# One-core hybrid block (gated delta rule + sparse attention + SwiGLU): five pieces of work moved or reshaped

## Chip, cores, metric

The kernel runs on one core of one Trainium2 chip. The metric is the device time of one execution in microseconds (us). Before the change it is 573.63 us, the median of three runs (571.04 to 574.39 us).

## The reference

One layer of a decoder block on x of shape (1, 256, 1024), float32. Two token mixers read the same normed input, their outputs are gated and merged, and a SwiGLU follows:

```python
h = rmsnorm(x, norm1_w)
proj = h @ w_in                      # one wide projection, cut into the parts of all heads
y_a = gated_deltanet(...)            # conv, l2-normed q/k, chunked delta rule, gated rmsnorm
y_b = native_sparse_attention(...)   # compressed, selected and window branches, shared bias
mixed = sigmoid(gate_a) * (y_a @ w_proj_a) + sigmoid(gate_b) * (y_b @ w_proj_b)
x = x + mixed @ w_out
h2 = rmsnorm(x, norm2_w)
x = x + (silu(h2 @ w_gate) * (h2 @ w_up)) @ w_down
```

What matters below: the attention's queries (8 heads of 128) are rmsnormed per token and head; the delta rule needs the inverse of unit-triangular 128x128 matrices, 16 of them (8 heads, two token tiles); the bias of the attention is a function of the distance of two tokens, one table per head; the delta rule's output o is rmsnormed per token and head.

## The kernel before, in words

**Weights as a stream.** All weights pass through SBUF in chunks of 1 MB (`CHUNKS`: gk, gq, gv 0..3, kc, vc, cmpk 0..3 mixed with nq 0..3, ks, kw, cmpv 0..3 mixed with vs, vw, gz, and so on to gu and dn). SyncE's queue issues the loads in that order into `raw` buffers (three in a ring, and `raw_ahead` for nq0 and nq2); a load waits until the chunk that held its buffer has been used. Each float32 chunk is split in two: ScalarE (ACT) copies it to `w_hi` (L629), VectorE (DVE) forms `w_lo = raw - w_hi` (L982), and TensorE (PE) does three products per tile (L1467 to L1469). There are two pairs `w_hi`/`w_lo`, so a chunk can be split only when the chunk two before it has been used by PE. Chunks of cmpk and cmpv are used unsplit (L1548).

**Slots.** Each engine runs its own list in program order, written out by hand: one slot per chunk, with two halves. In a slot, beside the chunk's own products, stand small pieces: a stage of the delta rule over four blocks b of four problems (`STAGE_AT`: row, kt, vt, knT, gram, kq, X4 ... o1; three banks in a ring carry the results between PE and DVE or ACT), a unit of the attention's softmax (`unit`), turns (transposes on PE) and norms. Semaphores couple the engines; a wait holds everything behind it on its engine.

**The diagonal blocks of the inverse.** After stage gram, GpSimd (POOL) sends the 16x16 diagonal blocks through DRAM (`sub_a`, `sub_m`), DVE inverts them (`solve_diagonal`, two parts), POOL sends them back (`sub_d`, `sub_dt`) and spreads them into `Db` and `DTb` by 16 DMAs (L589, L590). Stage X4, in the slot of cmpv0, waits for all of these.

**The bias.** DVE makes the table `bias_v` (8 x 384) in the opening. POOL writes it out 32 times to DRAM (`bias_rows`, L560), and reads it back skewed as `bias_g` (128 x 8 x 256, L576, four DMAs of 256 KB). It is first read much later, in the slot of vw.

**The queries.** The chunks nq0..3 are narrow: PE holds 128 weight columns and streams the 256 tokens of h, so the result stands head by head with tokens along the row. ACT copies it to `nqT` (L716) and squares it (L718). The sums of squares come from PE (`head_sums`, j = 2): four products with ones (L1661) after half 0 of ks, a copy by ACT (`csum_n`, L941), four turns after half 1 of ks. DVE makes the factor `rn` in the slot of cmpv1. Chunks of WIDE_KINDS (gz and later) are wide instead: PE holds 128 tokens of h and streams 512 weight columns; the token tile is the half.

**Opening.** x is normed (DVE, ACT), turned into channels (PE, eight tiles k), h is split tile by tile, and the first chunk's products run behind it.

**The factor of o.** DVE sums the squares of o (`output_sums`, L1144) in the slot of mga1, half 0, and makes the factor (`output_factor`) in half 1; then POOL scales o by it and by the gate (`scale_o`, L596 and L601), four blocks of each.

**End.** Four pieces of 512 columns of the output, each a DVE instruction (L1459) and a DMA on SyncE's queue.

Of the kernel before, what the change touches and what calls it, by code (L numbers as in the profile page):

```python
# [76 lines left out]
WIDE_KINDS = ("gz", "mga", "pa", "mgb", "pb")  # L77
# [116 lines left out]
def hybrid_block(nc, x, norm1_w, w_in, conv_w, a_log, dt_bias, gdn_norm_w, cmp_pe, cmp_w1, cmp_w2,  # L194
# [5 lines left out]
    with ctx:  # L200
# [33 lines left out]
        ones_nq = at("ones_nq", yb_at + 11 * KB + 128, [P, 32])  # L234
# [14 lines left out]
        nsq = [ar(5, f"nsq{i}", (P, 2, SEQ), off=i * 2 * KB) for i in range(4)]  # L249
# [44 lines left out]
        csum_n = at("csum_n", cursor[0] - 2 * KB, [P, 2 * SEQ])  # L294
# [55 lines left out]
        xss, xn_done = sem("xss"), sem("xn_done")  # L350
# [39 lines left out]
        def wait_bank(eng, n, t=0):  # L390
# [89 lines left out]
        def _(sp):  # L480
# [30 lines left out]
            for i in range(4):  # L511
                sp.wait_ge(fin, i + 1)
                t, c = i // 2, i % 2
                sp.dma_start(out[0].rearrange("(t p) d -> p t d", p=P)[:, t, c * 512:(c + 1) * 512],
                             out_sb[:, t, c * 512:(c + 1) * 512]).then_inc(out_done, 16)
            sp.wait_ge(out_done, 64)

        @block.gpsimd
        def _(pool):
# [87 lines left out]
        def _(act):  # L607
# [280 lines left out]
            for n in range(len(CHUNKS) + 1):  # L888
# [37 lines left out]
                for half in range(2):  # L926
# [10 lines left out]
                    for name in slot_stages(n, half):  # L937
                        gdn(name)
# [994 lines left out]
```

## Time and profile before

| | |
|---|---|
| median of the runs | 573.63 us |
| the profiled execution | 575.51 us, its span 573.7 us |
| mean granted TensorE clock | 0.993 of full speed |
| PE busy (matmul) | 563.1 us, 98% |
| DVE busy | 387.2 us, 67% |
| ACT busy | 305.1 us, 53% |
| POOL busy | 70.7 us, 12% |
| PE's share of the chain that ended last | 91% |

How to read it: the span runs from the first to the last instruction, and the execution has 1.8 us outside it. PE is busy nearly throughout, so the interesting things are the few microseconds in which it isn't, and those in which it is busy at a lower clock. A matmul's shown duration is longer than its step, since matmuls are pipelined; the step is read from the distance of starts, or from the chain, whose pieces do not overlap.

### The profile page before, as it was taken

The page shows a single profiled execution, that of the slowest core. Times are in us where ns is not written, and L with a number is a line of the kernel's source. Part 1 is how long each engine was busy: PE and PEld are TensorE (multiplying, and loading weights), DVE is VectorE, ACT ScalarE, POOL GpSimd, SP SyncE. Part 2 cuts the span into 40 slices and gives each one's busy share as a digit, 9 for nine tenths or more (in the row PEclk, how much of TensorE's full clock was granted, in tenths as well). Part 3 has the DMA queues.
Part 4 walks back from the last instruction along what each step waited for, and adds up shares of the span by engine and source line. Part 5 has one row for each costly group of instructions (what it writes and reads, how often), then busy time and mean ns, then how long its engine had stood idle before and what let it go on. Part 6 is the DMA issues. An engine that isn't in the chain of part 4 may idle for free.

```text
span 573.7 us, 9788 instructions
## 1 busy us (share of the span) xinstructions
PE 563.1 (98%) x3894; PEld 496.6 (87%) x3894; DVE 387.2 (67%) x617; ACT 305.1 (53%) x490; POOL 70.7 (12%) x85
## 2 busy tenths in 40 slices
PE   8999999999799999999999999999999999999997
PEld 8999999899698888888888888898888888888886
DVE  5879978846466653699875574757766656666664
ACT  4768568623345646655563634366555454554542
POOL 3122210964600000005200000000000000000000
PEclk9999999999799999999999999999999999999999
DMA  7944586289934433442354456575476665657631
GB/s 259 286 148 148 161 223 220 68 258 238 271 126 167 140 128 108 147 146 76 107 189 142 146 161 208 155 199 165 149 218 171 197 202 171 199 168 214 181 114 73
DMA packets 99254, 98.17 MB, mean 171 GB/s; under 512 B 4818, under 2 KB 83591, under 8 KB 99210
## 3 DMA queue, kind: packets, MB, share of 16 engines
q1 hardware_dynamic: 96896, 93.63, 52.7%
q0 software_dynamic: 1808, 2.78, 2.4%
q10 hardware_dynamic: 506, 1.14, 0.6%
q8 instruction: 31, 0.51, 0.4%
q14 instruction: 13, 0.11, 0.1%
HBM read 96.39 MB, written 1.84 MB: 171 GB/s over the span
## 4 chain that ended last, share of the span: by engine, by line
PE 91%; DVE 3%; DMA 3%; ACT 1%; issue 1%; ACTq 0%; DVEq 0%
PE ps L1467 18%; PE ps L1469 17%; PE ps L1468 17%; PE ps L1573 14%; PE ps L1576 7%; PE ps L1472 4%; PE ps L1693 4%; DMA raw<-in_w_in 2%; PE ps L1842 2%; PE ps L1816 2%; PE ps L1548 1%; PE ps L1718 1%; DMA rows_b<-in_cmp_pe 1%; DVE w_lo L982 1%; PE ps L1727 1%
## 5 line engine op out<-in xcount | busy, mean ns | idle before, releaser
L982 DVE TENSOR_TENSOR w_lo<-raw,w_hi 128x2048 fp32r<-128x2048 f32 x75 | 173.1, 2308 | 94.8 <-ACT w_hi L629 94.7
L629 ACT ACTIVATE w_hi<-raw 128x2048 fp32r<-128x2048 f32 x75 | 143.4, 1911 | 77.1 <-PE ps L1469 68.1
L1573 PE MATMUL ps<-h_both,w_hi 128*128 128x512 f32 x352 | 122.7, 397 | 0.2 <-issue 0.2
L1576 PE MATMUL ps<-h_both,w_lo 128*128 128x256 f32 x352 | 91.4, 280 | 0.3 <-DVE h_both L1008 0.3
L1467 PE MATMUL ps<-h_both,w_hi 128*128 128x256 f32 x272 | 77.8, 286 | 0.2 <-issue 0.2
L1468 PE MATMUL ps<-h_both,w_hi 128*128 128x256 f32 x272 | 76.9, 283 | 0.0
L1469 PE MATMUL ps<-h_both,w_lo 128*128 128x256 f32 x272 | 76.9, 283 | 0.0
L1573 PEld LDWEIGHTS ps<-h_both,w_hi 128*128 128x128 f32 x352 | 63.9, 188 | 13.8 <-issue 1.4
L1576 PEld LDWEIGHTS ps<-h_both,w_lo 128*128 128x128 f32 x352 | 66.4, 189 | 4.0 <-issue 0.6
L1467 PE MATMUL ps<-w_hi,h_both 128*128 128x512 f32 (+1 forms) x160 | 59.3, 370 | 3.1 <-issue 3.0
L1469 PE MATMUL ps<-w_hi,h_both 128*128 128x512 f32 (+1 forms) x160 | 56.7, 354 | 0.0
L1468 PE MATMUL ps<-w_lo,h_both 128*128 128x512 f32 (+1 forms) x160 | 56.6, 354 | 0.0
L1467 PEld LDWEIGHTS ps<-h_both,w_hi 128*128 128x128 f32 x272 | 52.1, 192 | 2.6 <-issue 2.5
L1468 PEld LDWEIGHTS ps<-h_both,w_hi 128*128 128x128 f32 x272 | 52.1, 192 | 0.0
L1469 PEld LDWEIGHTS ps<-h_both,w_lo 128*128 128x128 f32 x272 | 52.1, 192 | 0.0
L1467 PEld LDWEIGHTS ps<-w_hi,h_both 128*128 128x128 f32 x160 | 31.4, 196 | 8.7 <-issue 4.7
L1090 DVE SCALAR_TENSOR_TENSOR cacc<-cin,cols_a,cacc 128x256 f32<-128x256 f32 x72 | 35.0, 553 | 0.0
L1469 PEld LDWEIGHTS ps<-w_hi,h_both 128*128 128x128 f32 x160 | 31.4, 196 | 4.1
L1467 PE MATMUL ps<-w_hi,g_hi 128*128 128x512 f32 x88 | 34.4, 390 | 0.0
L1469 PE MATMUL ps<-w_hi,g_lo 128*128 128x512 f32 x88 | 34.3, 390 | 0.0
L1468 PEld LDWEIGHTS ps<-w_lo,h_both 128*128 128x128 f32 x160 | 31.5, 197 | 3.3
L1468 PE MATMUL ps<-w_lo,g_hi 128*128 128x512 f32 x88 | 34.3, 389 | 0.0
(381 smaller groups left out, 959.4 us busy)
## 6 DMA issues: line engine op xcount, KB each, us to landing
raw<-in_w_in SPq DMA_DIRECT2D x31, 1024.0 KB, 5.3
raw<-in_w_gate SPq DMA_DIRECT2D x22, 512.0 KB, 3.9
raw<-in_w_up SPq DMA_DIRECT2D x22, 512.0 KB, 5.2
raw<-in_w_down SPq DMA_DIRECT2D x11, 1024.0 KB, 4.9
raw<-in_cmp_w SPq DMA_DIRECT2D x8, 1024.0 KB, 7.3
raw<-in_w_proj_a SPq DMA_DIRECT2D x4, 1024.0 KB, 5.5
raw<-in_w_proj_b SPq DMA_DIRECT2D x4, 1024.0 KB, 5.0
raw<-in_w_out SPq DMA_DIRECT2D x4, 1024.0 KB, 5.1
```

Source lines behind the costliest of these rows:

```text
L629: nc.scalar.activation(w_hi[s % NSPL][:], raw[RAW_OF[n]][:], ACT.Copy).then_inc(hi_done, 1)
L982: nc.vector.tensor_tensor(w_lo[s % NSPL][:], raw[RAW_OF[n]][:], w_hi[s % NSPL][:].bitcast(f32), ALU.subtract).then_inc(lo_done, 1)
L1090: ins = nc.vector.scalar_tensor_tensor(acc, src[:, a, j:j + SEQ], tap(k, a, j), acc, ALU.mult, ALU.add)
L1467: pe.matmul(bank, lhs(lh), rhs(rh), start=start, stop=False)
L1468: pe.matmul(bank, lhs(lh), rhs(rl), start=False, stop=False)
L1469: return pe.matmul(bank, lhs(ll), rhs(rh), start=False, stop=stop)
L1472: return pe.transpose(o, i, ident[0:n, 0:n])
L1573: cross = lambda stop: pe.matmul(banks[part][:], hi[:, k, part * P:(part + 1) * P], h_both[:, :, k, :], start=(k == 0), stop=stop)
L1576: end = pe.matmul(banks[part][:, 0:SEQ], lo[:, k, part * P:(part + 1) * P], h_hi[:, k, :], start=False, stop=False)
L1693: mm = lambda q, lhsT, rhs, start=True, stop=True: pe.matmul(b4[:, q, :], lhsT, rhs, start=start, stop=stop)
L1816: last = pe.matmul(log_ps[:, a * SEQ:a * SEQ + w], nqT[:, h, t * P:(t + 1) * P], keys[:, h // 4, 0:w], start=True, stop=True)
L1842: last = pe.matmul(o, values[:, k, g, :], pt[j % 2][:, a * (t + 1) + k, :], start=False, stop=(a == 1 and k == t))
```

## The change

1. **Bias.** The write of `bias_rows` moves ahead, behind the squares of k and q; the four reads into `bias_g` move behind the 16 DMAs of the inverse's diagonal blocks.
2. **Queries.** nq becomes wide: the result stands token by token in PSUM. ACT squares it head by head with a running sum straight into `rn`'s column (L745 of the changed kernel, four instructions per half) and copies it to `nq_tok`; PE turns it back (`turn_q`, 16 turns in all, after nq2 and after ks), ACT copies the turned banks to `nqT` (`turned_q`). The head sums with j = 2 go (four products, four turns, the copy `csum_n`).
3. **Opening.** The second token tile's norm is cut by columns: 0 to 511 on ACT, 512 to 1023 on DVE behind the copy of `cols_b`; the turns of k = 0..3 wait for the first half alone. The first chunk's split of tiles 0..3 is cut in two.
4. **Factor of o.** `output_sums` moves from (mga1, half 0) to (gz3, half 1), `output_factor` from (mga1, 1) to (mga1, 0).
5. **Last turn of k.** Block 3 of stage kt moves from half 0 to half 1 of its slot, ahead of vt.
6. **End.** The last 512 columns of the output go out in two pieces of 256.

The diff, cut to its core:

```diff
-WIDE_KINDS = ("gz", "mga", "pa", "mgb", "pb")
+WIDE_KINDS = ("nq", "gz", "mga", "pa", "mgb", "pb")
...
+    name = STAGE_AT[where]
+    if name == "kt":
+        return [("kt", range(NB - 1))]
+    return ([("kt", (NB - 1,))] if name == "vt" else []) + [(name, range(NB))]
...
+OUT_PIECES = [(0, slice(0, 512)), (0, slice(512, 1024)), (1, slice(0, 512)), (1, slice(512, 768)), (1, slice(768, 1024))]
+TURN_Q = {(AT["nq", 2], 1): 0, (AT["ks", 0], 1): 1}
...
             act.wait_ge(rstd_ready, 1)
-            nc.scalar.activation(xn_sb[:, 1, 512:], x_sb[:, 1, 512:], ACT.Copy, scale=scol["x"][:, 5:6]).then_inc(xn_done, 1)
+            nc.scalar.activation(xn_sb[:, 1, 0:512], x_sb[:, 1, 0:512], ACT.Copy, scale=scol["x"][:, 5:6]).then_inc(xn_done, 1)
             act.wait_ge(raw_first, 16)
-            nc.scalar.activation(w_hi[0][:, 0:KT // 2, :], raw[0][:, 0:KT // 2, :], ACT.Copy).then_inc(first_hi, 1)
+            nc.scalar.activation(w_hi[0][:, 0:2, :], raw[0][:, 0:2, :], ACT.Copy).then_inc(first_hi, 1)
             for k in range(KT):
+                if k == 2:
+                    nc.scalar.activation(w_hi[0][:, 2:KT // 2, :], raw[0][:, 2:KT // 2, :], ACT.Copy).then_inc(first_hi, 1)
...
-                elif kind == "nq":
-                    nc.scalar.activation(nqT[:, 2 * i:2 * i + 2, :], bank, ACT.Copy).then_inc(copied, 1)
-                    act.wait_ge(copied, COPY_NO[n] + 1)
-                    nc.scalar.activation(nsq[i][:], nqT[:, 2 * i:2 * i + 2, :], ACT.Square).then_inc(nq_sq, 1)
...
+                if kind == "nq":
+                    act.wait_ge(half_done, 2 * n + 1 + t)
...
+                    for q in range(4):
+                        h = 2 * (i - 1) + q
+                        nc.scalar.activation(sc[0][:, q // 2, q % 2 * P:(q % 2 + 1) * P], bank[:, q * P:(q + 1) * P], ACT.Square,
+                                             accum_out=col["rn"][:, h, t:t + 1]).then_inc(nq_sq, 1)
+                    nc.scalar.activation(nq_tok[i // 2][:, t, :], bank[:], ACT.Copy).then_inc(copied, 1)
...
+            def turned_q(p):
+                for c in range(2):
+                    act.wait_ge(nq_turned, 2 * p + c + 1)
+                    nc.scalar.activation(nqT[:, 4 * p + 2 * c:4 * p + 2 * c + 2, :].rearrange("p h c -> p (h c)"), (log_ps, pv_ps)[c][:],
+                                         ACT.Copy).then_inc(nq_out, 1)
...
+                    if half == 0 and (n - 1, 1) in TURN_Q:
+                        turned_q(TURN_Q[n - 1, 1])
...
-                    if (n, half) == (AT["ks", 0], 1):
-                        act.wait_ge(csum_mm, 3)
-                        nc.scalar.activation(csum_n[:], ps[5][:], ACT.Copy).then_inc(csum_out, 1)
...
-            nc.vector.tensor_scalar(xn_sb[:, 1, 0:512], x_sb[:, 1, 0:512], scol["x"][:, 5:6], None, ALU.mult).then_inc(xn_done, 1)
             dve.wait_ge(pre_pe, 2)
             nc.vector.tensor_copy(cols_b[:], ps[7][:, P:P + NROWS]).then_inc(pre_dve, 1)
+            nc.vector.tensor_scalar(xn_sb[:, 1, 512:], x_sb[:, 1, 512:], scol["x"][:, 5:6], None, ALU.mult).then_inc(xn_late, 1)
...
+                    if (n, half) == (AT["gz", 3], 1):
+                        output_sums()
                     if (n, half) == (AT["mga", 1], 0):
-                        output_sums()
-                    if (n, half) == (AT["mga", 1], 1):
                         output_factor()
...
-            pe.wait_ge(xn_done, TT + 1)
-            to_channels(xn_sb, range(KT), tr_ready)
+            pe.wait_ge(xn_done, TT)
+            to_channels(xn_sb, range(KT // 2), tr_ready)
+            pe.wait_ge(xn_late, 1)
+            to_channels(xn_sb, range(KT // 2, KT), tr_ready)
...
+            def turn_q(p):
+                pe.wait_ge(copied, COPY_NO[AT["nq", 2 * p + 1]] + 1)
...
+                for c in range(2):
+                    if p == 1:
+                        pe.wait_ge(nq_out, c + 1)
+                    for q in range(4):
+                        h, t = 2 * c + q // 2, q % 2
+                        last = transpose((log_ps, pv_ps)[c][:, q * P:(q + 1) * P], nq_tok[p][:, t, h * P:(h + 1) * P])
+                    last.then_inc(nq_turned, 1)
...
                 elif m == W2_K:
                     pe.wait_ge(hid_done, 1)
-                    pe.wait_ge(rk_ready, 1)
+                    pe.wait_ge(nq_out, 4)
```

**POOL's queue around the diagonal blocks.** `sub_m` is the last step of the way out, the DMAs of `Db` and `DTb` are the way back. Before:

```order
L560 DMA bias_rows<-bias_v 256x1x384
L561 MEMSET DTb 128x2048
L564 TENSOR_TENSOR kn<-kn,cols 128x512 x4
L571 DMA sub_a<-ATb 16x16x16 x8
L573 DMA sub_m<-sub_a 128x256
L576 DMA bias_g<-bias_rows 32x8x256 x4
L578 DMA cmp_136<-in_cmp_w 128x4x128
L581 MEMSET Db 128x2048
L583 DMA sub_d<-sub_t 128x256
L585 DMA sub_dt<-sub_tt 128x256
```

After (the cut leaves out 14 DMAs of `Db` and `DTb` like the two shown):

```order
L563 MEMSET DTb 128x2048
L566 TENSOR_TENSOR kn<-kn,cols 128x512 x4
L573 DMA sub_a<-ATb 16x16x16 x8
L575 DMA sub_m<-sub_a 128x256
L577 DMA cmp_133<-in_cmp_w 128x4x128
L580 MEMSET Db 128x2048
L582 DMA sub_d<-sub_t 128x256
L584 DMA sub_dt<-sub_tt 128x256
...
L588 DMA Db<-sub_d 16x16x16
L589 DMA DTb<-sub_dt 16x16x16
L591 DMA bias_g<-bias_rows 32x8x256 x4
```

The four reads of the bias no longer stand between `sub_m` and the load of `cmp`; they are behind the last pair of `Db` and `DTb`, and the write of `bias_rows` has left this stretch.

**ACT from the split of nq3 (`w_hi_53<-raw_49`) to `hid_tok`.** The row `w_hi_52<-raw_51` is the split of ks, the next `w_hi_53<-raw_49` that of kw. Before:

```order
L629 ACTIVATE w_hi_53<-raw_49 128x2048
L716 ACTIVATE nqT<-ps 128x512
L718 ACTIVATE nsq_89<-nqT 128x512
L629 ACTIVATE w_hi_52<-raw_51 128x2048
L716 ACTIVATE nqT<-ps 128x512
L718 ACTIVATE nsq_90<-nqT 128x512
L629 ACTIVATE w_hi_53<-raw_49 128x2048
L936 ACTIVATE hid_tok<-ps 128x256
```

After:

```order
L631 ACTIVATE w_hi_53<-raw_49 128x2048
L631 ACTIVATE w_hi_52<-raw_51 128x2048
L769 ACTIVATE nqT<-ps 128x512 x2
L745 ACTIVATE sc_127,cols<-ps 128x128 x4
L747 ACTIVATE nq_tok_87<-ps 128x512
L745 ACTIVATE sc_127,cols<-ps 128x128 x4
L747 ACTIVATE nq_tok_87<-ps 128x512
L631 ACTIVATE w_hi_53<-raw_49 128x2048
L955 ACTIVATE hid_tok<-ps 128x256
```

Between the split of ks and that of kw stood two instructions; now twelve stand there (two copies of turned banks, twice four squares with a sum and a copy).

**DVE around the sums of o's squares, in the slot of mga1.** Before:

```order
L1276 TENSOR_TENSOR sc_131<-sc_131,s_fac 128x2x128
L1144 TENSOR_REDUCE cols<-kn 128x4 x4
L1265 SCALAR_TENSOR_TENSOR sc_130<-ps,cols,bias_g 128x2x128
L1266 TENSOR_REDUCE s_nm<-sc_130 128x2
L1273 RECIPROCAL s_fac<-s_se 128x2
L1274 TENSOR_TENSOR s_fac<-s_fac,gates 128x2
L1276 TENSOR_TENSOR sc_135<-sc_135,s_fac 128x512
L982 TENSOR_TENSOR w_lo_55<-raw_51,w_hi_53 128x2048
L1003 TENSOR_SCALAR cols<-cols 128x16
```

After:

```order
L1294 TENSOR_TENSOR sc_128<-sc_128,s_fac 128x2x128
L1019 TENSOR_SCALAR cols<-cols 128x16
...
L1283 SCALAR_TENSOR_TENSOR sc_127<-ps,cols,bias_g 128x2x128
L1284 TENSOR_REDUCE s_nm<-sc_127 128x2
L1291 RECIPROCAL s_fac<-s_se 128x2
L1292 TENSOR_TENSOR s_fac<-s_fac,gates 128x2
L1294 TENSOR_TENSOR sc_132<-sc_132,s_fac 128x512
L998 TENSOR_TENSOR w_lo_55<-raw_51,w_hi_53 128x2048
L1283 SCALAR_TENSOR_TENSOR sc_128<-ps,cols,bias_g 128x512
```

The ten small instructions of the factor, which begin with L1019, stand where the sums stood, one unit and one split earlier than before, so POOL's scaling of o may begin that much earlier.

## Rows read from the trace of the kernel before

**Rows 1.** Page, part 1: busy us, share of the span, instructions
```profile
PE 563.1 (98%) x3894; PEld 496.6 (87%) x3894; DVE 387.2 (67%) x617; ACT 305.1 (53%) x490; POOL 70.7 (12%) x85
```

**Rows 2.** PE's waits: line, releaser, us in total, times, longest
```profile
PE ps L1467 <- issue: 3.2, 2, 3.0
...
PE ps L1472 <- DVE sc L1276: 1.0, 1, 1.0
...
PE ps L1472 <- DVE AXb L1114: 0.6, 1, 0.6
```

**Rows 3.** Chain that ended last: start us, us, what
```profile
79.51 0.99 PE ps L1661 x8
...
114.99 3.77 PE ps L1693 x32
130.26 1.04 PE ps L1548 x16
131.32 11.22 DMA raw<-in_w_in
142.57 1.92 ACT w_hi L629
144.49 2.48 issue
...
152.43 1.33 PE ps L1661 x8
...
165.64 2.01 PE ps L1718 x64
...
340.40 0.87 PE ps L1472 x8
363.10 0.87 PE ps L1472 x8
```

**Rows 4.** Windows: PE, PEld, DVE, ACT, POOL busy, PEclk, DMA share, GB/s
```profile
147.00:152.40 5.40, 5.40 (x28) 5.18 (x30) 4.23 (x5) 0.94 (x2) 5.40 (x10) 0.50 1.10 325
```

**Rows 5.** DMAs issued 130.0 to 132.4 us: queue, count, size, median us to landing
```profile
raw<-in_w_in SPq DMA_DIRECT2D x1, 1024.0 KB, 11.2
bias_g<-bias_rows POOLq DMA_DIRECT2D x4, 256.0 KB, 5.5
```

**Rows 6.** DMA issued 146.5 to 148 us, the load of vs
```profile
raw<-in_w_in SPq DMA_DIRECT2D x1, 1024.0 KB, 8.4
```

**Rows 7.** DMAs issued 153.9 to 155.5 us, the last of the blocks
```profile
DTb<-sub_dt POOLq DMA_DIRECT2D x2, 16.0 KB, 5.3
```

**Rows 8.** Timeline of POOL: start us, us, engine, line, operation
```profile
129.74 2.33 POOL L576 DMA_DIRECT2D bias_g<-bias_rows  x4
...
154.65 0.57 POOL L590 DMA_DIRECT2D DTb<-sub_dt  x1
...
265.60 1.29 POOL L601 TENSOR_TENSOR kT<-kT,zs 128x512 f32<-128x512 f32 x1
```

**Rows 9.** Timeline of ACT
```profile
12.96 1.07 ACT L643 ACTIVATE w_hi<-raw 128x1024 fp32r<-128x1024 f32 x1
...
144.39 0.58 ACT L716 ACTIVATE nqT<-ps 128x512 f32<-128x512 f32 x1
...
147.58 0.37 ACT L936 ACTIVATE hid_tok<-ps 128x256 f32<-128x256 f32 x1
...
242.03 0.39 ACT L865 ACTIVATE sc<-sc,s_nm 128x128 f32<-128x128 f32 x1
...
242.41 0.39 ACT L865 ACTIVATE sc<-sc,s_nm 128x128 f32<-128x128 f32 x1
```

**Rows 10.** Timeline of DVE
```profile
255.46 0.43 DVE L1276 TENSOR_TENSOR sc<-sc,s_fac 128x256 f32<-128x256 f32 x1
255.80 2.46 DVE L1144 TENSOR_REDUCE cols<-kn 128x4 f32<-128x512 f32 x4
...
266.95 1.23 DVE L1276 TENSOR_TENSOR sc<-sc,s_fac 128x256 f32<-128x256 f32 x1
```

More of the change, by code:

```diff
@@ L248, in hybrid_block @@
         csum = ar(6, "csum", (P, 2 * SEQ), off=4 * KB)
-        nsq = [ar(5, f"nsq{i}", (P, 2, SEQ), off=i * 2 * KB) for i in range(4)]
+        nq_tok = [ar(5, f"nq_tok{i}", (P, TT, 2 * CW), off=i * 4 * KB) for i in range(2)]
         ya_hi, ya_lo = ar(5, "ya_hi", (P, KT, SEQ), f32r), ar(6, "ya_lo", (P, KT, SEQ), f32r)
@@ L510, in _ @@
                 load_chunk(n)
-            for i in range(4):
+            for i, (t, c) in enumerate(OUT_PIECES):
                 sp.wait_ge(fin, i + 1)
[L513 to L516, printed above, removed]
+                sp.dma_start(out[0].rearrange("(t p) d -> p t d", p=P)[:, t, c], out_sb[:, t, c]).then_inc(out_done, 16)
+            sp.wait_ge(out_done, 16 * len(OUT_PIECES))
         @block.gpsimd
@@ L590, in _ @@
                 pool.dma_start(rows(DTb, s), cells(sub_dt, s)).then_inc(diag_in, 16)
+            for a in range(4):
+                pool.dma_start(bias_g[32 * a:32 * a + 32, :, :],
+                               bass.AP(bias_rows.tensor, P - 1 - 32 * a, [[383, 32], [384 * 32, HEADS], [1, SEQ]])).then_inc(bias_in, 16)
             pool.wait_ge(m_out, TURN_KW + 1)
@@ L792, in row_differences, with gdn @@
                 ins.then_inc(g_out[u % GRING], 1)
-            def gdn(name):
+            def gdn(name, blocks):
                 if name == "row":
                     return
-                for b in range(NB):
+                for b in blocks:
                     u = stage_use(name, b)
@@ L936, in _ @@
                         nc.scalar.activation(hid_tok[:], ps[6][:, 0:CW], ACT.Copy).then_inc(hid_raw, 1)
-                    for name in slot_stages(n, half):
-                        gdn(name)
-                    if (n, half) == (AT["ks", 0], 1):
-                        act.wait_ge(csum_mm, 3)
-                        nc.scalar.activation(csum_n[:], ps[5][:], ACT.Copy).then_inc(csum_out, 1)
+                    for name, blocks in slot_stages(n, half):
+                        gdn(name, blocks)
                     if n - 1 in (AT["cmpk", 3], AT["cmpv", 3]) and half == 1:
@@ L1102, in by_chunk, with gdn @@
                 return col[name][:].rearrange("p (c a) t -> p a t c", a=2)
-            def gdn(name):
-                for b in range(NB):
+            def gdn(name, blocks):
+                for b in blocks:
                     u = stage_use(name, b)
@@ L1412, in _ @@
                             split_lo(m)
-                    for name in slot_stages(n, half):
-                        gdn(name)
+                    for name, blocks in slot_stages(n, half):
+                        gdn(name, blocks)
                     if (n, half) in SOLVES:
@@ L1452, in _ @@
                         nc.vector.tensor_tensor(yb_lo[:, 2 * b:2 * b + 2, :], nqT[:, 2 * b:2 * b + 2, :], yb_hi[:, 2 * b:2 * b + 2, :].bitcast(f32), ALU.subtract).then_inc(yb_lo_done, 1)
-            for i in range(4):
+            for i, (t, c) in enumerate(OUT_PIECES):
                 if i < 3:
@@ L1658, in head_sums @@
                         pe.wait_ge(csum_out, j)
-                    squares, one = (nsq, ones_nq[:]) if j == 2 else (csq, ones_sq[:, 0:32])
                     for i in range(4):
-                        last = pe.matmul(ps[5][32 * i:32 * i + 32, :], one, squares[i][:].rearrange("p a c -> p (a c)"), start=True, stop=True)
+                        last = pe.matmul(ps[5][32 * i:32 * i + 32, :], ones_sq[:, 0:32], csq[i][:].rearrange("p a c -> p (a c)"), start=True, stop=True)
                     last.then_inc(csum_mm, 1)
@@ L1686, in gdn @@
                     return
-                for b in range(NB):
+                for b in blocks:
                     u = stage_use(name, b)
@@ L1879, in _ @@
                         last.then_inc(rows_mm, 1)
-                    for name in slot_stages(n, half):
-                        gdn(name)
+                    for name, blocks in slot_stages(n, half):
+                        gdn(name, blocks)
                     for m in slot_misc(n, half):
```

79 lines of the change are left out of this document (40 added, 39 removed).

## Prediction

> **What bounds the kernel now.** I read the page first: PE is busy for 563.1 of 573.7 us [rows 1], so nothing but PE's own work, its clock and its few waits can move the time. The table of PE's waits then names the gaps: one of 3.0 us, one of 1.0 behind DVE's scaled probabilities, one of 0.6 behind DVE's part of stage kt [rows 2]; the rest lie in the first and last microseconds. The chain shows what the 3.0 us are: the load of ks is issued at 131.32 and lands 11.2 us later, ACT splits it at 142.57, DVE after it, and PE starts ks at 144.49 + 2.48 = 146.97 [rows 3]. At the same moment the four reads of the bias are in flight, 1 MB in all [rows 5, 8]. Behind the wait PE runs at a granted clock of 0.50, 1.2 instead of 2.4 GHz, at least until 152.4 [rows 4]. So one late load costs twice. The shorter waits of 1.0 and 0.6 us left the clock as it was.
>
> **The change, part by part.** The sum is made against the profiled execution (575.5 us, span 573.7), 1.9 us above the median of the runs; I carry the difference over to the median.
>
> *The wait before ks: -3.0.* The reads of the bias leave the stretch 129.7 to about 140 and the write of 384 KB leaves the one before it. The same kind of load takes 8.4 us beside other traffic in another place [rows 6]; at 5.5 to 8.4 us ks lands at 136 to 139 instead of 142.5. PE comes to ks at about 143.5, and the split needs 1.9 (ACT) [rows 3] and some 2.3 more on DVE. Bounds: -3.0 if it is in time, 0 if the reads were not the cause.
>
> *The low clock: -2.9.* The 24 matmuls of ks, half 0, took 152.43 - 146.97 = 5.46 us. At full clock the step of such a matmul is (130.26 - 118.76) / 96 = 0.120 us, from the 96 between the end of stage kq (114.99 + 3.77) and cmpk2 [rows 3], so 2.88 for 24: 2.6 lost. The head sums behind them took 1.33 us against 0.99 at full clock [rows 3]: 0.3. Bounds: 0, if a wait as long stays, to -2.9.
>
> *Wide queries: -1.2.* Before, 192 matmuls of 256 columns, 192 x 0.120 = 23.0 us. After, 96 of 512 columns. Their step: between the turns at 340.40 + 0.87 and 363.10 stand 96, 21.83 / 96 = 0.227 us [rows 3], 21.8 in all. -1.2; at worst nothing, where the narrow matmuls beside small pieces gain less.
>
> *Turns and head sums: +0.3.* Out go 0.99 us of sums and four turns; a turn is 0.87 / 8 = 0.11 us [rows 3]: -1.4. In come 16 turns, +1.7. Bounds 0 to +0.8.
>
> *New work on ACT: +1.3 in two new waits.* A square with a running sum, 128x128, repeats every 242.41 - 242.03 = 0.38 us, as the exponentials with a sum do [rows 9]. Four and a copy of 0.58 are 2.0 to 2.1 us per half, four times, plus two copies per turned pair (1.2). Before, the nq copy and square cost half of that. They stand in ACT's list ahead of the split of kw and of `hid_tok`. I step it through, PE's starts taken from the steps above: nq3 ends at about 142.4, the last evacuation at 144.5, kw's split at 146.4, `hid_tok` at 146.8. PE, no longer held before ks, ends ks half 0 at about 146.4 and then wants `hid_tok`, which before was ready at 147.95 with PE late anyway [rows 9]. Wait: 0.5, up to 1.5 if ks lands at 139, since the same list is served in order. Second, `turned_q(1)` stands behind the split of vs, and vs, issued at about 144, may need 8.4 us again [rows 6]: landed 152.3, split 154.2, turned 155.4, while PE wants to start W2_K at 154.5 or so. Behind W2_K on PE stand kw half 1 and X4. Wait: 0.8, bounds 0 to 2.
>
> *The diagonal blocks: 0, but the cover is thin.* Before, the last `DTb` is issued at 154.65 and lands 5.3 us later, at 160.0 [rows 7, 8]; PE starts X4 at 165.64 [rows 3]. The items above and the opening bring X4 forward by 5.1 us, to 160.5. POOL's queue is shorter by the bias write, and the loads that disturb it less, so the blocks come 0.5 to 2 us earlier. The reads of the bias now follow the last pair and share the DMA engines with it. I take 0; late by s us it costs s, and about 3 more if the clock falls as above. The bias itself, landing by some 165, isn't wanted before the slot of vw: free.
>
> *Kt: 0.* The 0.6 us wait [rows 2] goes, since a chunk's half stands between block 3 and the first three. But DVE now has block 3's two instructions ahead of vt's four, and vt's third block needs its bank. The wait moves by one stage. Bounds -0.6 to +0.6.
>
> *Opening: +0.4.* PE doesn't wait for the norm there (no such row in [rows 2]), so the earlier half of x buys nothing. The half split moved between the first two and the next tiles of h takes half of 1.07 us on ACT [rows 9]; h's tiles 2 to 7 and the next chunk's split come 0.5 later. A part is hidden. Bounds -0.5 to +0.7.
>
> *Factor of o: -0.2.* The sums' 2.46 us of DVE [rows 10] leave a full stretch for a lighter one, and the factor's ten small instructions (about 2 us) come a unit earlier. That attacks the 1.0 us wait for the probabilities. But look at what made them late: a multiply that takes 0.43 us elsewhere takes 1.23 us at 266.95 [rows 10], while POOL works on o [rows 8]. POOL will now start 6 us earlier and run beside the split of mga3 and the next unit. The mechanism: each DVE instruction with two SBUF operands waits for a POOL instruction, about 0.8 us each; three such waits take back the 2 us that the factor freed, and the wait stays. I take a small gain; bounds -1.0 (wait gone) to +0.5 (moved sums make the split of mga1 late). The Trainium skill says this flatly ("SBUF — State Buffer", section "SBUF: two separate sides"): DVE and POOL share one port pair under an exclusive lock, held for a whole instruction, and the loser blocks. By that rule the term would be +0.2, not -0.2; the multiply's 1.23 us agrees with it.
>
> *End: 0.* Smaller last piece, one more DMA issue, about 0.6 us as on POOL [rows 8], which the earlier half hides; bounds -0.2 to +0.4.
>
> Sum: -3.0 - 2.9 - 1.2 + 0.3 + 1.3 + 0 + 0 + 0.4 - 0.2 + 0 = -5.3. The profiled execution would be 570.2, the median 573.6 - 5.3 = 568.3 us.
>
> **Rivals.**
> - *Forecast* (0.40): as summed; 566.8 to 570.0.
> - *No new waits* (0.16): ks and vs land in the 5.5 us of the reads' own rows [rows 5], ACT keeps up, the opening costs nothing, the 1.0 us wait goes: -3.0 - 2.9 - 1.2 + 0.3 - 0.8 = -7.6, 566.0; 564.5 to 566.8. For it: ACT is busy only 53% [rows 1]. Against: its list is served in order, and just here it is full.
> - *The port keeps the wait* (0.14): the sum with +0.2 to +0.9 for the factor's part: 568.7 to 569.4, up to 570.0 with the spread. The rule cited above is this rival.
> - *ks stays late* (0.22): the bias isn't what delays it, or cmp and the earlier queue do as much. Then ks lands at 140 or later, ACT's longer list comes behind it, PE waits 2 us or more, and part of the low clock returns: gain 0.5 to 3.5, 570 to 573. For it: kw and two more loads were slow too [rows 6]. Against: 1 MB of bias in the same 11 us [rows 5].
> - *The blocks become the bound* (0.08), the case on the other side: the last `DTb`, now with 1 MB of bias reads behind it, lands after PE reaches X4 at 160.5. A wait of s costs s + 3 once the clock falls. From s = 2.3, a landing at 162.8, the kernel is slower than before; at 168.5 by 1%. 573.5 to 580.
>
> **How the numbers follow.** A measurement of this kernel tells about 1%, 5.7 us, from no change. Below 567.9 lie the second case and some 0.18 of the first, with 0.02 of the third: faster 0.36. Over 579.4 lies half of the last case: slower 0.04. Same 0.60. The range 565.0 to 572.0 leaves out the last case, a third of the second and a quarter of the fourth. The likeliest case's own range is 566.8 to 570.0.
>
> **What would show it.** Right: load of ks landing within 8.5 us; no wait of 3 us and no stretch at clock 0.50 near 145; PE waits of 0.3 to 1.5 us before the product with `hid_tok` and before W2_K, both behind ACT; X4 starting at 160 to 161; 96 matmuls of nq at 0.227 us; a wait near vt in place of that in kt; multiplies of 1.0 to 1.5 us on DVE while POOL scales o. Wrong: ks landing after 141, a wait for `DTb` before X4, a stretch of 0.50 anywhere but the end, or an opening that ends earlier than before (PE's first chunk waits for x after all, which the table of waits can't show if a matmul's wait is drawn as its length).

## The result and the profile after

The changed kernel takes 575.47 us, the median of 20 runs (574.19 to 577.08). The kernel before, run beside it 20 times, takes 573.35 us (571.04 to 574.66). The ratio is 1.0044, with a 95% interval of 1.0031 to 1.0057: slower by 0.44%, where 568.3 us and a gain of 0.9% were forecast. The forecast range, 565.0 to 572.0, missed it.

Executions of one kernel differ by several us, and the mean granted TensorE clock tells a part of it. In the 15 runs of before that stand beside the first experiments, those at 0.999 or 1.000 took 571.4 to 572.5 us, those at 0.996 or 0.997 took 572.6 to 575.7. All 20 runs of the changed kernel are at 0.991 to 0.997. None has a full clock.

The profiled execution of after takes 575.41 us, span 573.4. Its page, part 1:

```profile
span 573.4 us, 9642 instructions
...
PE 561.9 (98%) x3802; PEld 491.7 (86%) x3802; DVE 388.2 (68%) x619; ACT 308.5 (54%) x522; POOL 71.4 (12%) x84
```

PE's waits in it (engine, tile, line, releaser: total us, times, longest):

```profile
PE ps L1812 <- issue: 4.0, 1, 4.0
PE ps L1489 <- DMA rows_b<-in_cmp_pe: 1.1, 1, 1.1
...
PE ps L1592 <- issue: 0.6, 1, 0.6
PE ps L1489 <- DVE AXb L1132: 0.5, 1, 0.5
...
PE ps L1484 <- DVE zs L1338: 0.2, 1, 0.2
```

Against [rows 2]: the 3.0 us before ks are gone, and so is the 1.0 us behind the scaled probabilities, for which 0.2 behind DVE's `zs` came in, from the moved sums. The wait in kt is now one in vt, 0.5 instead of 0.6. A new one of 4.0 us stands at L1812, which is W2_K.

The new wait in the timeline (start, us, engine, line, operation; in brackets the idle time before and what ended it). First SP's and POOL's issues, then ACT, then PE:

```profile
131.38 6.25 SPq L503 DMA_DIRECT2D raw<-in_w_in  x2
144.42 0.37 SPq L503 DMA_DIRECT2D raw<-in_cmp_w  x1
144.88 0.54 SPq L503 DMA_DIRECT2D raw<-in_w_in  x1
...
144.12 0.59 POOL L588 DMA_DIRECT2D Db<-sub_d  x1 [1.99 <-DMA sub_dt<-sub_tt]
...
152.49 0.56 POOL L589 DMA_DIRECT2D DTb<-sub_dt  x1
153.04 2.32 POOL L591 DMA_DIRECT2D bias_g<-bias_rows  x4
```

```profile
137.86 1.92 ACT L631 ACTIVATE w_hi<-raw 128x2048 fp32r<-128x2048 f32 x1 [4.06 <-DMA raw<-in_w_in]
...
140.68 0.28 ACT L745 ACTIVATE sc<-ps 128x128 f32<-128x128 f32 x1
...
140.95 0.27 ACT L745 ACTIVATE sc<-ps 128x128 f32<-128x128 f32 x1
...
146.70 0.41 ACT L955 ACTIVATE hid_tok<-ps 128x256 f32<-128x256 f32 x1
...
155.52 1.91 ACT L631 ACTIVATE w_hi<-raw 128x2048 fp32r<-128x2048 f32 x1 [3.47 <-DMA raw<-in_w_in]
157.34 1.07 ACT L769 ACTIVATE nqT<-ps 128x512 f32<-128x512 f32 x2
```

```profile
154.22 0.28 PE L1486 MATMUL ps<-w_hi,h_both 128*128 128x256 f32 x1
158.50 1.87 PE L1812 MATMUL ps<-cmp,hid 128*15 128x128 f32 x8 [4.00 <-issue]
160.30 0.58 PE L1484 MATMUL ps<-w_hi,h_both 128*128 128x256 f32 x1
...
165.67 0.33 PE L1734 MATMUL ps<-Db,ATb 64*64 64x64 f32 x4
```

ks is issued at 131.38, and ACT can split it at 137.86: 6.5 us instead of 11.2 [rows 3]. That part worked. vs is issued at 144.88 and lands at 155.52, 10.6 us later. ACT's list has the copies of the turned queries (L769) behind the split of vs. They begin at 157.34, and PE, done with kw half 0 at 154.50, waits until 158.50. The waits table calls it "issue" and names no releaser; the end of L769's second copy, 157.34 + 1.07 = 158.41, fits, and x1 below tests it.

The chain that ended last (start, us, what) shows the wide queries too: 48 of their products between the end of stage kq at 119.41 and cmpk2 at 130.32.

```profile
119.41 0.23 PE ps L1484
...
130.32 1.00 PE ps L1567 x16
```

Then the clock. Stretches of after (us, busy time and instructions of each engine, granted clock, DMA share, GB/s):

```profile
core 0: us, PE busy (x) PEld busy (x) DVE busy (x) ACT busy (x) POOL busy (x), PEclk, DMA share, GB/s
147.00:152.40 5.40, 5.40 (x48) 5.40 (x47) 4.81 (x8) 1.56 (x4) 5.40 (x10) 1.00 1.12 300
154.50:158.50 4.00, 0.00 (x0) 0.03 (x1) 2.10 (x5) 2.88 (x3) 0.86 (x2) 0.75 1.13 245
158.50:165.00 6.50, 6.50 (x40) 5.48 (x44) 4.24 (x17) 0.22 (x1) 0.00 (x0) 0.63 0.77 165
165.00:170.00 5.00, 5.00 (x99) 4.43 (x92) 0.00 (x0) 3.07 (x6) 0.00 (x0) 1.00 0.62 188
```

147 to 152.4, which was at 0.50 before [rows 4], is at 1.00. The low clock has moved to the new wait and the stretch behind it, where PE works for part of 158.5 to 165 at 1.2 instead of 2.4 GHz. W2_K takes 1.87 us and kw half 1 4.4, where 1.05 and 3.1 are usual. X4 starts at 165.67; in [rows 3] it was 165.64. What the change won up to 154.5 is spent by 165.7.

### The profile page after: what moved, and what is told of

It reads as the page before. It is cut to its first block, busy times and chain, and to the rows that moved or that the text cites. A ratio compares the mean times of both kernels' runs of the same rounds, so it can differ in the third digit from the quotient of the medians.

```text
span 573.4 us, 9642 instructions
## 1 busy us (share of the span) xinstructions
PE 561.9 (98%) x3802; PEld 491.7 (86%) x3802; DVE 388.2 (68%) x619; ACT 308.5 (54%) x522; POOL 71.4 (12%) x84
## 4 chain that ended last, share of the span: by engine, by line
PE 94%; DVE 2%; issue 1%; DMA 1%; ACT 1%; ACTq 0%; DVEq 0%
PE ps L1484 19%; PE ps L1486 18%; PE ps L1485 18%; PE ps L1592 14%; PE ps L1595 7%; PE ps L1489 4%; PE ps L1709 4%; PE ps L1870 2%; PE ps L1844 2%; PE ps L1567 1%; DMA rows_b<-in_cmp_pe 1%; PE ps L1734 1%; PE ps L1743 1%; PE ps L1867 1%; DVE out_sb L1477 0%
## 5 line engine op out<-in xcount | busy, mean ns | idle before, releaser
L631 ACT ACTIVATE w_hi<-raw 128x2048 fp32r<-128x2048 f32 x75 | 143.5, 1913 | 79.7 <-PE ps L1486 68.0
L1595 PE MATMUL ps<-h_both,w_lo 128*128 128x256 f32 x352 | 91.3, 280 | 0.3 <-DVE h_both L1024 0.3
L1592 PEld LDWEIGHTS ps<-h_both,w_hi 128*128 128x128 f32 x352 | 63.9, 188 | 14.1 <-issue 1.9
L1484 PE MATMUL ps<-w_hi,h_both 128*128 128x512 f32 (+1 forms) x192 | 71.7, 373 | 0.3 <-DVE zs L1338 0.2
L1595 PEld LDWEIGHTS ps<-h_both,w_lo 128*128 128x128 f32 x352 | 66.4, 189 | 4.0 <-issue 0.6
L1486 PE MATMUL ps<-w_hi,h_both 128*128 128x512 f32 (+1 forms) x192 | 68.7, 358 | 0.0
L1485 PE MATMUL ps<-w_lo,h_both 128*128 128x512 f32 (+1 forms) x192 | 68.5, 357 | 0.0
L1484 PE MATMUL ps<-h_both,w_hi 128*128 128x256 f32 x208 | 59.6, 286 | 0.2 <-issue 0.2
L1485 PE MATMUL ps<-h_both,w_hi 128*128 128x256 f32 x208 | 58.8, 283 | 0.0
L1486 PE MATMUL ps<-h_both,w_lo 128*128 128x256 f32 x208 | 58.8, 283 | 0.0
L1484 PEld LDWEIGHTS ps<-w_hi,h_both 128*128 128x128 f32 x192 | 36.9, 192 | 7.8 <-issue 2.3
L1484 PEld LDWEIGHTS ps<-h_both,w_hi 128*128 128x128 f32 x208 | 39.8, 192 | 2.3 <-issue 2.0
L1486 PEld LDWEIGHTS ps<-w_hi,h_both 128*128 128x128 f32 x192 | 36.8, 192 | 5.4
L1485 PEld LDWEIGHTS ps<-w_lo,h_both 128*128 128x128 f32 x192 | 37.0, 193 | 4.4
L1485 PEld LDWEIGHTS ps<-h_both,w_hi 128*128 128x128 f32 x208 | 39.9, 192 | 0.0
L1486 PEld LDWEIGHTS ps<-h_both,w_lo 128*128 128x128 f32 x208 | 39.9, 192 | 0.0
```

Source lines behind the costliest of these rows:

```text
L631: nc.scalar.activation(w_hi[s % NSPL][:], raw[RAW_OF[n]][:], ACT.Copy).then_inc(hi_done, 1)
L1484: pe.matmul(bank, lhs(lh), rhs(rh), start=start, stop=False)
L1485: pe.matmul(bank, lhs(lh), rhs(rl), start=False, stop=False)
L1486: return pe.matmul(bank, lhs(ll), rhs(rh), start=False, stop=stop)
L1592: cross = lambda stop: pe.matmul(banks[part][:], hi[:, k, part * P:(part + 1) * P], h_both[:, :, k, :], start=(k == 0), stop=stop)
L1595: end = pe.matmul(banks[part][:, 0:SEQ], lo[:, k, part * P:(part + 1) * P], h_hi[:, k, :], start=False, stop=False)
```

## Experiments

Two yardsticks serve in all of them, both from PE's rows in the timeline. S is the time from the first of the eight products that end the first chunk (L1646, at 17.93 in after) to the first product of X4 (165.67): 147.74. It leaves out how late the opening's small loads land. The tail is the time from X4 to the end of PE's last product, 404.26 in after.

My theory A after reading the trace: the loss is the wait for `turned_q(1)`, which stands on ACT behind a split that waits for a load, and the half clock behind it. Rivals: the moved bias itself is what loses, by the traffic it puts beside vs and the blocks; or the wait, once removed, only moves on to X4.

**x1_turned_first.** The changed kernel with ACT's two pieces in the other order:

```diff
                         evacuate(n - 1, "a" if n in GU_OPENING else "ab")
+                    if n == AT["kw", 0]:
+                        turned_q(1)
...
-                    if half == 0 and (n - 1, 1) in TURN_Q:
+                    if half == 0 and (n - 1, 1) in TURN_Q and n != AT["kw", 0]:
```

> The changed kernel with one thing moved: ACT copies the second pair of turned queries (turned_q(1)) before it splits vs, instead of behind that split. Theory A (the loss is PE's wait of 4.0 us before W2_K, behind a split that waits for the load of vs, and the half clock that follows it): that wait goes to under 0.5 us, no stretch at half clock between 150 and 170, PE's kw half 1 takes 2.9 us instead of 4.4; gain 4.0 + 3.4 = 7.4 us on 575.5: 568.1, range 567 to 569.5. Theory B (the wait only moves on): PE reaches X4 near 159 while the last DTb lands near 159 to 161, waits there 1 to 2 us or more and the clock falls anyway: 570 to 575.

Measured: 570.49 us (568.78 to 570.86), ratio to before 0.9943 (0.9923 to 0.9963). ACT in its trace:

```profile
153.32 1.07 ACT L769 ACTIVATE nqT<-ps 128x512 f32<-128x512 f32 x2
157.25 1.91 ACT L631 ACTIVATE w_hi<-raw 128x2048 fp32r<-128x2048 f32 x1 [2.86 <-DMA raw<-in_w_in]
```

vs is as slow as in after (issued 146.24, landed 157.25, 11.0 us), and nobody minds: W2_K starts at 155.79 without a wait. S is 141.36, 6.4 less than in after. PE waits nowhere near X4. Theory A holds, and the rival of the moved wait falls for this execution. The time is 5.0 below after (5.8 by the two ratios to before) and not 7.4: above the range of theory A, and by its number alone in that of theory B, but the wait that B expected isn't there. One part of the miss is the half clock, which I took at 3.4 and which is worth 2.2 (below). Another is in the opening: in this execution PE waited 2.3 us for `rows_b` and the clock of 8 to 20 us was 0.86. The two executions at 0.999 and 1.000 took 568.8 and 569.3.

**x4_bias_only, x2_queries_only, x3_all_but_queries.** Item 1 of the change alone; item 2 alone; everything but item 2. The first two as diffs against before, cut to one line each of what is in the change's diff:

```diff
+            pool.dma_start(bias_rows, bias_v[:].unsqueeze(1).to_broadcast([HEADS, 32, 384])).then_inc(bias_out, 16)
             pool.dma_start(levels[:], c_levels).then_inc(levels_in, 16)
...
-WIDE_KINDS = ("gz", "mga", "pa", "mgb", "pb")
+WIDE_KINDS = ("nq", "gz", "mga", "pa", "mgb", "pb")
```

> The kernel before with the bias move alone. Theory A: as the kernel without wide queries, minus what opening, factor, kt and end bring together (within 0.7 us of it): 568.5 to 571. Load of ks lands in 6 to 8 us instead of 11.2. Theory B: 573 to 577, with a wait for vs's split or for DTb in the place of that before ks.

> The kernel before with the wide queries alone (the reads of the bias stay in their old place, opening, factor, kt and end as before). Theory A: wide queries are worth about -0.9 us on PE, but they bring the wait for turned_q(1) before W2_K. The wait before ks stays (bias reads still ahead of it), and ACT's list is later with it, so both waits are there or one of them long: no faster than before, 573.5 to 579. Theory B (the bias move makes vs late, the queries alone are harmless): no wait over 1 us before W2_K, 571.5 to 573.

> The changed kernel without the wide queries: bias reads late, opening, factor, kt and end as changed, nq narrow with head sums. Theory A (the bias move works, the queries spoil it): W2_K waits for nothing of ACT's, the wait before ks is under 1 us, no half clock near 150: 573.4 - 3 to 5 + 0.4: 568.5 to 571. Theory B (the moved bias is what loses, by the traffic it puts beside vs and the blocks): a wait over 1 us somewhere in 140 to 170, 573 to 577.

| kernel | median, us | ratio to before (95%) | S | tail |
|---|---|---|---|---|
| bias alone | 570.07 | 0.9949 (0.9930 to 0.9968) | 142.41 | 404.50 |
| all but queries | 569.96 | 0.9942 (0.9924 to 0.9960) | 142.58 | 404.61 |
| queries alone | 573.56 | 1.0020 (1.0004 to 1.0036) | 145.75 | 404.48 |

The bias move alone is worth 0.5% and holds the clock: 4 of its 5 executions are at 1.000, within 569.8 to 570.2. The queries, as the change has them, cost. Their waits, with the bias reads in the old place:

```profile
PE ps L1478 <- ACT nq_tok L742: 2.2, 1, 2.2
...
PE ps L1801 <- issue: 1.4, 1, 1.4
...
PE ps L1483 <- DVE sc L1287: 1.0, 1, 1.0
...
PE ps L1885 <- ACT hid_tok L950: 0.4, 1, 0.4
```

Three waits are there: 2.2 before ks (the table names ACT's `nq_tok`, which ends at 146.27; DVE's half of the late ks ends at 146.18), then `hid_tok` 0.4, then W2_K 1.4. The clock of this execution is 1.0 throughout: behind a wait of 2.2 us it stayed. So theory A holds in all three, and the bias as the culprit falls. But compare W2_K's start: 158.61 here, 158.50 in after. It goes by the landing of vs, at 155.63 here and 155.52 there. While the queries hang behind that load, what the bias move brings PE forward only makes its wait longer, 4.0 for 1.4, until the clock falls. In bias alone vs lands even later (issued 144.82, split at 157.43, 12.6 us) with no wait, for no one needs anything that stands behind its split.

**x7_blocks_held.** What makes vs late? Here POOL starts the 16 DMAs of the blocks only once vs has landed:

```diff
             pool.wait_ge(d_init, 2)
+            pool.wait_ge(raw_in[RAW_OF[AT["vs", 0]]], 16 * loads_before(AT["vs", 0]))
             for s in range(NSUB):
```

> The changed kernel with POOL holding the 16 DMAs of the diagonal blocks until vs has landed. Theory A (vs is late because these small DMAs and cmpv0 and cmpv1 run beside it): vs lands in 6 to 8 us instead of 10.6, W2_K waits 1.5 us or less; in exchange the blocks start at about 152, end near 166, and PE waits at X4 for 3 to 6 us with the clock down: 575 to 580. Theory B (the two cmpv loads alone delay vs): vs lands in 10 us or more, W2_K waits 3.5 to 4.5 us as before, and X4 waits too: 580 or more.

PE's waits, and ACT's split of vs in the timeline:

```profile
PE ps L1735 <- DMA DTb<-sub_dt: 7.2, 1, 7.2
...
PE ps L1813 <- issue: 1.6, 1, 1.6
```

```profile
154.53 1.91 ACT L632 ACTIVATE w_hi<-raw 128x2048 fp32r<-128x2048 f32 x1 [1.04 <-DMA raw<-in_w_in]
```

One execution, 581.6 us. vs, issued at 146.33, lands 8.2 us later instead of 10.6, and W2_K's wait falls from 4.0 to 1.6. X4 waits 7.2 us in exchange, where 3 to 6 were expected, so the time is above theory A's range. cmpv0 was issued 0.46 us ahead of vs, as in after, so it is the small DMAs beside vs that this edit takes away, and 2.4 us go with them. The bias reads, which this edit also puts off, are not the cause: in x8 below, where they had been issued at 128.93, vs took 11.4. The small DMAs are not all of it either: in [rows 6] they ran beside vs too, and it took 8.4 (see the failed step below).

**x6_filled_wait and x11_filled_short.** What does the half clock cost by itself? Products of the identity into an unread part of a bank take the place of the idle time:

```diff
                     pe.wait_ge(hid_done, 1)
+                    for _ in range(36):
+                        pe.matmul(pt_ps[:, 3 * P:], ident[:], ident[:], start=True, stop=True)
                     pe.wait_ge(nq_out, 4)
```

> The changed kernel with 36 products of the identity with itself (128x128, into a part of a PSUM bank that nobody reads) ahead of PE's wait for the turned queries at W2_K: some 3.7 us of filler in place of idle time. Theory A (the 4.0 us of idle time made the clock fall, and the half clock behind it costs 3.4 us by itself): W2_K still starts near 158.5, kw half 1 takes 3.1 us instead of 4.4, gain 3.4: 572.1, range 571.3 to 573. Theory B (the half clock there has another cause than the idle engine): no gain, 575 to 576.

I had sized the filler by a transpose, some 0.1 us. A product of this form took 8.2 / 36 = 0.228 us, so it ran past the wait: 578.0 us, W2_K at 162.67. The clock stayed at 1.00, and kw half 1 took 3.13. The mistake gave the unit for the second one, with 17:

> The changed kernel with 17 filler products ahead of W2_K's wait instead of 36. One took 8.2 / 36 = 0.228 us, so 17 take 3.9 us, as long as the wait. Theory A (the half clock by itself costs 2.1 us: from the start of W2_K to that of X4 165.67 - 158.50 = 7.17 us in the changed kernel, 167.71 - 162.67 = 5.04 us behind the long filler): W2_K starts at 158.5, X4 at 163.5, 575.5 - 2.1 = 573.4, range 572.8 to 574. Theory B (my first 3.4 us): 572.1. Theory C (the clock falls anyway): 575.5.

PE in the timeline, and the stretch behind the wait:

```profile
157.75 0.61 PE L1809 MATMUL ps<-ident 128*128 128x128 f32 x4
...
158.48 1.05 PE L1814 MATMUL ps<-cmp,hid 128*15 128x128 f32 x8
...
163.53 0.27 PE L1734 MATMUL ps<-Db,ATb 64*64 64x64 f32 x2
```

```profile
158.50:165.00 6.50, 6.50 (x98) 5.49 (x100) 4.17 (x17) 1.97 (x4) 0.00 (x0) 1.00 0.83 174
```

573.73 us (573.20 to 574.99). W2_K starts at the same 158.5 as in after, the clock is 1.00, and S is 145.53, 2.2 less. That is the price of the half clock; the wait itself is the other 4.2 between this S and x1's 141.36. It is also a repair of a kind: work that computes nothing won 1.7 us (1.5 by the two ratios to before). "TensorE: Matmul & The Clock Gate" in the Trainium skill (section "Terms") puts the penalty at the throttled time times one half. From the two stretches of after, the time at half clock is (0.25 x 4.0 + 0.37 x 6.5) / 0.5 = 6.8 us, so 3.4 by that rule. The runs show less, 2.2: some 2 us of it lay in the idle time before 158.5, where it costs nothing.

**x8_before_again.** The kernel before once more, one execution, 570.85 us:

> The kernel before, once more, for its stretch around the load of ks. Theory A (the profiled execution, above all of its other runs, had a longer stall than most): wait before ks of 1 to 2.5 us and a clock that stays up behind it, 571.5 to 573. Theory B (the 3.0 us and the half clock are its usual course): both return, 574 to 576.

PE's first product of ks, and the stretch around it:

```profile
145.33 0.35 PE L1469 MATMUL ps<-w_hi,h_both 128*128 128x256 f32 x1 [1.06 <-issue]
```

```profile
143.00:152.40 9.40, 8.34 (x76) 6.61 (x75) 6.75 (x8) 4.05 (x6) 7.74 (x14) 1.00 0.80 207
```

The wait before ks is 1.06 us here, not 3.0, and the clock behind it is full. S is 143.50; in the execution of [rows 3] it was 148.14. The stall on which 5.9 us of my sum rested was a bad draw. But x8 is a good one, and lies below theory A's range: of the 91 other runs of before in these sessions (median 572.9) one is below 570.85, and three are above the 575.51 of the profiled execution.

**x5_best.** Items 1, 2 (with `turned_q(1)` ahead), 4 and 5; opening and end as before.

> Bias reads late, wide queries with turned_q(1) ahead of the split of vs, factor of o and last turn of k moved; opening and end as in the kernel before. Theory A (the queries are worth -1.0 once their wait is gone, the factor -0.8 by the wait of 1.0 us that disappears, the opening edit costs 0.4): against the kernel with the bias move alone (570.1) -1.0 - 0.7: 568.4, range 567.8 to 569.2, no PE wait over 0.6 us after the opening. Theory B (port: POOL's scaling of o beside DVE gives the factor's gain back elsewhere): 569.2 to 570.

568.77 us (567.78 to 570.35), ratio 0.9924 (0.9900 to 0.9949): it beats both kernels, before by 0.8%. S is 141.36 and the tail 403.74. Its profiled execution waited 2.0 us for `rows_b` and lost clock in the opening; the six executions at 0.999 or 1.000 took 567.8 to 569.2.

**x10_factor_back.** x5 with the factor of o in its old place (item 4 undone).

```diff
-                    if (n, half) == (AT["gz", 3], 1):
-                        output_sums()
                     if (n, half) == (AT["mga", 1], 0):
+                        output_sums()
+                    if (n, half) == (AT["mga", 1], 1):
                         output_factor()
```

> The kernel of x5 with the factor of o in its old place (sums in mga1 half 0, factor in mga1 half 1). Theory A (the move is worth 0.8: it takes PE's wait of 1.0 us for the scaled probabilities and costs one of 0.2): the wait of 1.0 us is back, 568.8 + 0.8: 569.6, range 569 to 570.2. Theory B (POOL's beginning earlier beside DVE gives it back, as the rival of the port has it): within 0.2 of x5's 568.8.

```profile
PE ps L1490 <- DVE sc L1294: 1.0, 1, 1.0
```

570.53 us (568.72 to 571.80). Seven of its 12 executions were at 0.996 or 0.997, so the 1.8 us between the medians overstate it. The tail tells it: 404.60 against 403.74, 0.86 for the factor. The rival of the port is wrong in its result, but not in its mechanism. In after, DVE beside POOL:

```profile
259.75 1.68 DVE L1294 TENSOR_TENSOR sc<-sc,s_fac 128x512 f32<-128x512 f32 x1
261.36 3.12 DVE L998 TENSOR_TENSOR w_lo<-raw,w_hi 128x2048 fp32r<-128x2048 f32 x1
...
262.41 3.23 POOL L603 TENSOR_TENSOR kT<-kT,zs 128x512 f32<-128x512 f32 x1
```

The multiply takes 1.68 where 0.69 is usual, the split 3.12 where 2.29 is. The stalls are there, but POOL starts six microseconds earlier (258.46 for 264.48), and they fall on instructions for which PE doesn't wait. The rule of the Trainium skill that the prediction cites ("SBUF — State Buffer", section "SBUF: two separate sides") agrees with these durations and says nothing of the time.

**x9_more_busy and x12_opening_back_in.** x5 with two more of the opening's filler products; and the same with the changed opening (item 3) put back.

```diff
             pe.wait_ge(ones_set, 2)
-            keep_busy(20)
+            keep_busy(22)
```

> The kernel of x5 with 22 instead of 20 of the opening's keep-busy products. Theory A (the executions of x5 at clock 0.996 to 0.997, 569.4 to 570.4 us, lost the clock in the opening, behind the 2.0 us in which PE waits for rows_b; the ones at 0.999 to 1.0 are 567.8 to 569.2): the wait shrinks to 1.4 us or less and nearly all executions are at 0.999 or more, 568.2, range 567.7 to 569. Theory B (the spread has another cause): 568.8 as before, with the same spread.

> The kernel of x9 (22 keep-busy products, old opening and end) with the changed opening put back in; the end stays old. Theory A (the changed opening costs 0.4 us on PE by the 20th microsecond, and it is also what brings the wait of 0.54 instead of 0.19 us near 398, where DVE starts a split 0.47 instead of 0.11 us behind ACT's): 568.6 + 0.4 + 0.35 = 569.4, range 568.9 to 570, that wait at 0.5 us or more. Theory B (the wait near 398 comes with the changed end): 0.19 there, 569.0.

x9: 568.62 us (567.84 to 569.25), ratio 0.9924 (0.9905 to 0.9944), all six executions at 0.999 or 1.000. But x12 has the same 22, its profiled execution waited 2.2 us for `rows_b`, and six of its 12 executions are at 0.996 or 0.997. So whether two products help isn't settled; the lateness of `rows_b` varies by itself. x12 takes 569.88 us, ratio 0.9949 (0.9929 to 0.9969). Its waits:

```profile
PE ps L1494 <- DMA rows_b<-in_cmp_pe: 2.2, 1, 2.2
PE ps L1739 <- DMA DTb<-sub_dt: 1.2, 1, 1.2
...
PE ps L1597 <- issue: 0.5, 1, 0.5
```

The 0.5 us at L1597 near 400 came back with the opening, as theory A had it; x9 has 0.2 there. And X4 waited 1.2 us for the last `DTb`: the rival on the other side, seen at last in one execution. The cover over the diagonal blocks is as thin as the prediction feared.

## Why the prediction was wrong, point by point

| term | forecast | measured |
|---|---|---|
| wait before ks | -3.0 | -3.0 against the profiled execution, -1.1 against x8 |
| low clock near 147 | -2.9 | -2.7 (148.14 - 143.50 less the two waits' difference), and 0 against x8 |
| wide queries with turns and sums | -0.9 | -0.95 (S of bias alone less S of x5, without kt's 0.1) |
| new waits on ACT | +1.3 | +4.0 |
| half clock behind them | none | +2.2 |
| kt | 0 | -0.1 (0.5 for 0.6) |
| opening | +0.4 | +0.4 (0.2 from the turns of x to the start of S, 142.58 - 142.41 in S), and 0.35 more near 400 |
| factor of o | -0.2 | -0.86 |
| end | 0 | +0.15 |

The end is read from span less PE's end: 573.4 - 569.93 = 3.47 in after, 567.5 - 564.24 = 3.26 in x5, 569.0 - 565.68 = 3.32 in x8. From x8's span, 569.0, the right-hand terms give 569.0 - 1.1 - 0.95 + 4.0 + 2.2 - 0.1 + 0.75 - 0.86 + 0.15 = 573.1; after's is 573.4.

- **The step that failed** is "Second, `turned_q(1)` stands behind the split of vs" with "Wait: 0.8, bounds 0 to 2". The mechanism was right to the instruction, and so was PE's time at W2_K, 154.5. The size was wrong: 4.0. I gave vs the 8.4 us of [rows 6]; it took 10.6, and it was issued 0.9 later than I had it. That row likely owed its 8.4 us to the very stall that the change removes. In the kernel before (rows below) vs was issued only once ks, which was late, had been split, 2.9 us behind cmpv0. With ks in time it follows cmpv0 by 0.5 us (144.42 and 144.88 in after). The traces go with that distance: 8.4 us at 2.9, 9.4 at 2.0 (x2), and 10.4 to 12.6 in the eleven traces at 0.5 to 1.0, all with POOL's small DMAs beside. The small DMAs start 2.2 us earlier in after (144.12 for 146.30), but vs is issued 2.1 us earlier too, so that doesn't tell the two kernels apart. With them held and the distance at 0.5, vs took 8.2. No run changes the distance alone, so how much of the 10.6 is cmpv0's stays open. One late load thus became another. The prediction's "kw and two more loads were slow too" points at [rows 6], which shows vs alone.

```profile
144.02 0.37 SPq L498 DMA_DIRECT2D raw<-in_cmp_w  x1
146.95 0.37 SPq L498 DMA_DIRECT2D raw<-in_w_in  x1
...
146.30 0.59 POOL L589 DMA_DIRECT2D Db<-sub_d  x1 [4.66 <-DMA sub_dt<-sub_tt]
```

- **The clock was left out of that term.** I wrote "about 3 more if the clock falls" for a wait at X4 and not for the same engine's wait six microseconds earlier. This wait cost its length and the half clock: 4.0 + 2.2.
- **The base was wrong.** The profiled execution stood above all its own runs (575.5 against 571.0 to 574.4), and I carried over the whole 5.9 us that its stall had cost. Against x8 only 1.1 of them were there to win. The gain of bias alone on the medians is 572.51 - 570.07 = 2.4 us, and 572.3 - 570.1 = 2.2 among the executions at 0.999 or 1.000, so the usual stall lies between the two profiled ones; no further trace of before shows it. On the medians, 6.2 for 1.3 at W2_K and 2.4 for 5.9 before ks are 8.4 us of error, and the other terms take 0.3 back: 8.1, where 575.47 - 573.35 + 5.3 = 7.4 were missing.
- **Right:** ks landing within 8.5 us, no wait and full clock near 145, the queries' products at (130.32 - 119.41) / 48 = 0.227 us, no wait for the blocks in after, the wait for kt in vt, the opening's price. The wait before `hid_tok` did not come, and not for ACT's sake. Its squares repeat every 0.27 us or less instead of the 0.38 of [rows 9], but it has `hid_tok` at 147.1, later than the 146.8 of the forecast. PE came later still: it started ks at 144.29 for 143.5 and wants `hid_tok` at 147.27 for 146.4.
- **The factor** was sized too small out of the belief that the port's stalls would land on the same wait.

## What to carry to other kernels

When a new instruction goes into an engine's list, ask which load the instruction ahead of it waits for, and bound that load by the slowest row of its kind in the trace, not by the nearest; ask too whether the change itself alters when that load is issued. A wait of 3 us or more on TensorE is costed with the half clock behind it, by these traces. And before a sum is built on one stall of a profiled execution, compare that execution with its own runs: if it stands above them all, the stall is likely larger there than usual, and one that stands below them all sizes it too small.

## What the runs showed of the hardware

- **The clock after a wait.** It stayed full behind waits of 1.06, 1.2, 1.4, 1.6 and 2.2 us in the middle of the kernel, and fell with those of 3.0, 4.0 and 7.2. In the opening it fell in the five profiled executions that waited 2.0 to 2.7 us for `rows_b`, and stayed in the others, at 0.5 to 1.8.
- **A split that starts late.** Near 400 us DVE begins a split 0.47 us after ACT's half has ended in after (398.37 + 1.92 = 400.29 to 400.76), and 0.11 us after it in before (399.01 + 1.91 = 400.92 to 401.03). It is the same code, 380 us behind the opening. After first, then before:

```profile
398.37 1.92 ACT L631 ACTIVATE w_hi<-raw 128x2048 fp32r<-128x2048 f32 x1
400.76 2.29 DVE L998 TENSOR_TENSOR w_lo<-raw,w_hi 128x2048 fp32r<-128x2048 f32 x1 [1.24 <-ACT w_hi L631]
```

```profile
399.01 1.91 ACT L629 ACTIVATE w_hi<-raw 128x2048 fp32r<-128x2048 f32 x1
401.03 2.29 DVE L982 TENSOR_TENSOR w_lo<-raw,w_hi 128x2048 fp32r<-128x2048 f32 x1 [0.87 <-ACT w_hi L629]
```

The wait of PE behind it is 0.53 to 0.56 us in all seven traces with the changed opening and 0.18 to 0.19 in all seven with the old one. x12 and x9 differ in the opening alone, so it is the opening that does it; by what path is open.
- **What runs beside a large load.** 1 MB of vs, issued 0.5 us behind another load of 1 MB, took 8.2 us without the blocks' small DMAs beside it (one trace). With them it took 10.4 to 12.6 us at 0.5 to 1.0 us behind (eleven traces), 9.4 at 2.0 and 8.4 at 2.9 (one each).
